# Encoder layer on one core: the order of the work in front of the experts, with the gate projection in pieces between attention's steps

## The reference, cut to what matters

```python
n = rms_norm(h, mix_norm_g)
z = n @ w_in                     # 1024 x 2336, all groups' projections side by side
gq, gk, gv, gr, zf, zb, aq, ak, av = split_cols(z, IN_SPLITS)
# gated linear attention (GLA), 4 heads, chunks of 64, forward and backward
g_fwd = log_sigmoid(zf @ w_gf + b_gf) / 16      # zf, zb: 16 columns each
g_bwd = log_sigmoid(zb @ w_gb + b_gb) / 16
o = rms_norm(o_f + o_b, head_g) * silu(gr)      # gr: 512 columns, the output gate
# softmax attention, 8 query heads on 2 key heads, rotary positions
qf = axial_rope(rms_norm(qh, q_g)) * DH ** -0.5
kf = axial_rope(rms_norm(kh, k_g))
h = h + concat(o_gla, o_att) @ w_out            # 1024 x 1024
# mixture of experts: top 4 of 32, clamped SwiGLU, then a last norm
h = h + moe_ffn(rms_norm(h, ffn_norm_g), ...)
y = rms_norm(h, final_norm_g)
```

## Time and profile before

| | |
|---|---|
| median of 3 runs | 1078.08 us (1078.02 to 1078.13) |
| the profiled execution's own time | 1077.54 us |
| its span | 1075.5 us |
| PE busy | 984.4 us (92%) |
| DVE, ACT, POOL busy | 224.2, 117.7, 15.5 us |
| DMA | 421.4 MB, mean 392 GB/s |
| chain that ended last | PE 53%, DMA 39%, DVE 4%, ACT 2% |

### The profile page before, as it was taken

How to read it: one execution, slowest core, us unless ns; L and a number is a source line. 1 busy time by engine, 2 the same in 40 slices (tenths; PEclk the granted TensorE clock), 3 DMA queues, 4 the chain that set the end, 5 groups by cost and what they waited for, 6 DMA issues and landing times.

```text
span 1075.5 us, 13809 instructions
## 1 busy us (share of the span) xinstructions
PE 984.4 (92%) x5833; PEld 424.4 (39%) x5833; DVE 224.2 (21%) x522; ACT 117.7 (11%) x233; POOL 15.5 (1%) x19
## 2 busy tenths in 40 slices
PE   7997989999999999988888988898988888999996
PEld 4644543444444444333333333333333333333432
DVE  1577342111111111111111101111111111101112
ACT  1053130000000000000000000000000000000002
POOL 0010010000000000000000000000000000000000
PEclk9998899999999999999999999999999999999999
DMA  9924748999999999999999999999999999999995
GB/s 330 295 108 206 313 157 347 427 428 427 426 428 427 428 429 429 428 428 428 429 428 428 427 428 428 429 428 428 429 429 429 429 428 428 428 428 427 427 423 225
DMA packets 33675, 421.40 MB, mean 392 GB/s; under 512 B 4944, under 2 KB 5456, under 8 KB 7568
## 3 DMA queue, kind: packets, MB, share of 16 engines
q1 hardware_dynamic: 33648, 421.02, 93.6%
HBM read 419.95 MB, written 1.05 MB: 391 GB/s over the span
## 4 chain that ended last, share of the span: by engine, by line
PE 53%; DMA 39%; DVE 4%; ACT 2%; issue 1%; POOL 0%; SPq 0%; POOLq 0%
DMA ring<-in_w_dram 38%; PE bank L1534 22%; PE bank L1576 13%; PE bank L1148 4%; PE bank L1460 3%; PE bank L1448 3%; PE bank L1362 1%; PE bank L1558 1%; ACT work L606 1%; PE bank L1494 1%; PE bank L1354 1%; PE bank L1383 1%; ACT work L537 1%; DMA h<-in_x_dram 0%; PE bank L1290 0%
## 5 line engine op out<-in xcount | busy, mean ns | idle before, releaser
L1534 PE MATMUL bank<-ring,work 128*64 128x512 f32 x2016 | 457.4, 598 | 45.4 <-DMA ring<-in_w_dram 44.3
L1534 PEld LDWEIGHTS bank<-ring,work 128*64 128x64 f32 x2016 | 167.4, 136 | 315.3 <-issue 212.5
L1576 PE MATMUL bank<-ring,work 128*64 128x512 f32 x992 | 219.7, 595 | 15.1 <-ACT work L606 15.1
L1039 DVE TENSOR_SCALAR work<-bank 128x512 f32<-128x512 f32 x31 | 21.4, 692 | 697.4 <-PE bank L1534 697.4
L1576 PEld LDWEIGHTS bank<-ring,work 128*64 128x64 f32 x992 | 69.0, 137 | 145.8 <-issue 128.9
L603 ACT ACTIVATE work<-work 128x512 f32<-128x512 f32 x31 | 19.6, 632 | 512.1 <-DVE work L1039 512.1
L1460 PE MATMUL bank<-work 64*128 64x512 f32 x256 | 63.6, 615 | 0.7 <-ACT work L638 0.7
L1448 PE MATMUL bank<-work,tok 128*128 128x64 bf16 x992 | 46.7, 193 | 0.0
L1448 PE MATMUL bank<-work 128*128 128x64 bf16 x496 | 45.2, 194 | 0.0
L1448 PEld LDWEIGHTS bank<-work,tok 128*128 128x128 bf16 x992 | 43.7, 98 | 0.0
L614 ACT ACTIVATE work<-bank 128x512 f32<-128x512 f32 x31 | 18.5, 597 | 214.8 <-PE bank L1576 214.8
(11 more groups left out here) (212 smaller groups left out, 505.3 us busy)
## 6 DMA issues: line engine op xcount, KB each, us to landing
ring<-in_w_dram SPq DMA_DIRECT2D x187, 2048.0 KB, 33.1
ring<-in_w_in_dram SPq DMA_DIRECT2D x8, 1168.0 KB, 17.3
ring<-in_w_dram SPq DMA_DIRECT2D x6, 1024.0 KB, 33.2
work<-in_w_dram SPq DMA_DIRECT2D x2, 2048.0 KB, 11.3
ring<-in_w_out_dram SPq DMA_DIRECT2D x2, 1024.0 KB, 13.2
ring<-in_w_out_dram SPq DMA_DIRECT2D x1, 2048.0 KB, 19.5
h<-in_x_dram SPq DMA_DIRECT2D x2, 512.0 KB, 4.3
out_dram<-tok SPq DMA_DIRECT2D x4, 256.0 KB, 2.2
```

The costliest lines, as they stand in the source:

```text
L1039: nc.vector.tensor_scalar(glu, bank[2][:, :], LIMIT, None, ALU.min).then_inc(S.glu_ready, 1)
L1534: last = mm(bank[(2, 5)[g]][j * CAP:(j + 1) * CAP, :], xg[:, k * CAP:(k + 1) * CAP], chunk[:, r, g * FF + j * FG:g * FF + (j + 1) * FG], s ...
L1576: last = mm(bank[6][j * CAP:(j + 1) * CAP, :], hidT[:, r, s * CAP:(s + 1) * CAP], chunk[:, r, j * 512:(j + 1) * 512], start=s == 0 and r == 0,
```

## The change

The same arithmetic, in another order, and in other banks:
- **Pass 1.** The low-rank columns are made with the activations stationary (128 wide) and the 32 weight columns moving, for both t, and come out with tokens on partitions (bank 1). DVE scales them by the row's 1/rms (`zg_t`), PE turns them back (`turn_zg`, two transposes), DVE copies them into `zg`. Attention's q of t = 1 leaves pass 1 and becomes eight matmuls behind it, with `turn_zg` after the first and `gates()` after the fourth.
- **Gate pass.** Pass 3 is cut into pieces of 4, 2 and 2 k (`gate_pass`), which lie between attention's steps; ACT copies its result out (`gate_out`, Copy in place of Sigmoid), the sigmoid comes later, after attention.
- **`turn_qk`** moves into pass 2, behind k = 5; the rotation on DVE (`rotated(0)`, `rotated(1)`) moves ahead of the scans of the gate chain; ACT's squares for q and k go into a buffer of their own (`sq`) and ahead of Abs, Exp, Ln.
- **GLA's products** on DVE are cut up (`decayed_near`, `decayed_queries`, `decayed_keys`, `carried_keys`) and lie between the softmax steps. `gla_first(0)` comes after `turn_weights(2)`.
- **Output projection.** Attention's part (`out_att`) lies in part between attention's steps and GLA's outputs; all of it, for t = 1 too, is ahead of the wait for `ogla_sb`.
- **Waits.** The router's and GLA's late constants have a semaphore of their own (`late_in`), so `const_in` counts four transfers in place of six. The early chunks wait for `mix01_used` in place of `attT_ps`.

```diff
-CONSTS = 6
+CONSTS = 4
+LATE = 2
...
-            sp.wait_ge(S.attT_ps, ATT_PAIRS)
+            sp.wait_ge(S.mix01_used, 1)
...
+            act.wait_ge(S.raw_sb, 3 * TILES)
+            nc.scalar.activation(sq, raw, ACT.Square).then_inc(S.raw_sq, 1)
...
+            def gate_out():
+                act.wait_ge(S.pass3, KD)
+                for t in range(TILES):
+                    nc.scalar.activation(sg[:, t, :], bank[MIX[t]][:, :], ACT.Copy, scale=stat[:, 4 + t:5 + t]).then_inc(S.gr_sb, 1)
...
+            for t in range(TILES):
+                nc.scalar.activation(tok[:, t, GLA_V:D], sg[:, t, :], ACT.Sigmoid).then_inc(S.gr_sig, 1)
...
+            dve.wait_ge(S.raw_sb, 3 * TILES)
+            step(rotated(1))
+            dve.wait_ge(S.raw_sq, 1)
+            step(nc.vector.tensor_reduce(stat[:, 28:48], sq.rearrange("p t (h d) -> p (t h) d", d=DH), AX.X, ALU.add))
+            mean_eps(stat[:, 8:28], stat[:, 28:48], DH).then_inc(S.hvar_done, 1)
+            step(nc.vector.tensor_tensor(rot, rot, swp, ALU.add))
             dve.wait_ge(S.gln, 1)
             step(nc.vector.scalar_tensor_tensor(gM, gM, 0.0, gA, ALU.min, ALU.subtract))
+            dve.wait_ge(S.hrstd_done, 1)
...
+            decayed_near()
+            row_maxima(0)
+            row_maxima(1)
+            normalise(0)
+            decayed_queries()
+            weights_out(0)
+            decayed_keys()
+            normalise(1)
+            carried_keys()
+            row_maxima(2)
+            weights_out(1)
+            normalise(2)
+            row_maxima(3)
+            weights_out(2)
+            normalise(3)
+            dve.wait_ge(S.late_in, 16 * LATE)
+            gla_scores(0)
+            weights_out(ATT_PAIRS - 1)
+            gla_scores(1)
...
-                put(bank[2][0:2 * RANK, 0:SEQ], w[:, C_ZG:C_AQ], xT(k), True)
+                for t in range(TILES):
+                    last = put(bank[1][:, t * 2 * RANK:(t + 1) * 2 * RANK], xT(k, t), w[:, C_ZG:C_AQ], t == 0)
...
+            for k in range(KD):
+                last = mm(bank[4][:, :], xT(k, 1), w_in_sb[:, k, C_AQ:C_AK], start=k == 0, stop=k == KD - 1)
+                if k == 0:
+                    turn_zg()
+                if k == 3:
+                    gates()
+            last.then_inc(S.pass1, 1)
...
-            pe.wait_ge(S.rms_sb, 1)
+            pe.wait_ge(S.gates_sb, 1)
             for k in range(KD):
                 for t in range(TILES):
                     last = mm(bank[6 + t][:, :], xT(k, t), w_in_sb[:, k, C_GV:C_GR], start=k == 0, stop=k == KD - 1)
                 last.then_inc(S.pass2, 1)
-                if k == 0:
-                    gates()
+                if k == 5:
+                    turn_qk()
+
+            def gate_pass(k0, k1):
+                if k0 == 0:
+                    pe.wait_ge(S.gqk_sb, 2)
+                for k in range(k0, k1):
...
-            pe.wait_ge(S.raw_sb, 3 * TILES)
-            for k in range(KD):
-                for t in range(TILES):
-                    last = mm(bank[3 + t][:, :], xT(k, t), w_in_sb[:, k, C_GR:C_ZG], start=k == 0, stop=k == KD - 1)
-                last.then_inc(S.pass3, 1)
-                if k == KD - 3:
-                    turn_qk()
...
             scores(0)
-            gla_first(0)
             scores(1)
+            gate_pass(0, 4)
             turn_weights(0)
-            gla_second(0)
+            gate_pass(4, 6)
             values(0)
             scores(2)
             turn_weights(1)
-            gla_first(1)
+            gate_pass(6, 8)
             values(1)
             scores(3)
             turn_weights(2)
+            gla_first(0)
+            gla_second(0)
+            values(2)
+            pe.wait_ge(S.w_out_att_in, 32)
+            out_att(0, (0,))
+            turn_weights(3)
+            gla_first(1)
             gla_second(1)
-            turn_weights(3)
-            values(2)
+            values(3)
+            out_att(0, (1,))
+            pe.wait_ge(S.mix_done, 2)
             gla_outputs(0)
-            gla_outputs(1)
-            values(3)
+            gla_outputs(1).then_inc(S.mix01_used, 1)
             gla_outputs(2)
             gla_outputs(3).then_inc(S.ogla_ps, 1)
+            pe.wait_ge(S.attT_sb, 2)
+            out_att(0, (2, 3))
+            out_att(1, range(4)).then_inc(S.att_used, 1)
```

More of the change, by code:

```diff
@@ L178, in encoder_layer @@
         av = front(TILES, ATT_KV)
+        at_gv = front.at
         gv = front(TILES, GLA_V)
@@ L187, in encoder_layer @@
         picked = front(TILES, EXPERTS + TOP_K)
+        zg_t = front(TILES, 2 * RANK)
         assert front.at <= WORK
@@ L194, in encoder_layer @@
         rms = reuse(SEQ)
+        sq = Carve(work, at_gv)(TILES, QK)
+        assert at_gv + TILES * QK <= at_sg + SEQ
         reuse = Carve(work, at_rot)
@@ L796, in _ @@
-            step(last)
-            for d in range(2):
-                nc.vector.tensor_tensor(pairs(gB, d), pairs(gB, d), q2, ALU.mult).then_inc(S.gla_ready, 1)
-            k4 = k2.rearrange("p (g c i) -> p g c i", g=2, i=CHUNK)
-            for d in range(2):
-                last = nc.vector.tensor_tensor(kk[:, 2 * d:2 * d + 2, :, :].rearrange("p g s i -> p g s i")[:, :, 0:5:2, :],
-                                               gM[:, 2 * d:2 * d + 2, :].rearrange("p g (c i) -> p g c i", i=CHUNK)[:, :, d:d + 3, :],
-                                               k4[:, :, d:d + 3, :], ALU.mult)
@@ L805, in _, with decayed_near, decayed_queries @@
-            step(last)
+            def decayed_near():
+                dve.wait_ge(S.exp_done, 2)
+                for d in range(2):
+                    nc.vector.tensor_tensor(pairs(gX, d), pairs(gX, d), q2, ALU.mult).then_inc(S.gla_ready, 1)
+                    nc.vector.tensor_tensor(pairs(gA, d), pairs(gA, d), k2, ALU.mult).then_inc(S.gla_ready, 1)
+            dec = stat[:, 128:128 + 4 * CHUNKS]
+            def decayed_queries():
+                dve.wait_ge(S.exp_done, 4)
+                for d in range(2):
+                    last = nc.vector.tensor_copy(dec[:, 8 * d:8 * d + 8].rearrange("p (c o) -> p c o", o=1),
+                                                 chunked(gB, d)[:, :, edge[d]:edge[d] + 1])
+                step(last)
+                for d in range(2):
+                    nc.vector.tensor_tensor(pairs(gB, d), pairs(gB, d), q2, ALU.mult).then_inc(S.gla_ready, 1)
@@ new lines, in decayed_keys @@
+            def decayed_keys():
+                k4 = k2.rearrange("p (g c i) -> p g c i", g=2, i=CHUNK)
+                for d in range(2):
+                    last = nc.vector.tensor_tensor(kk[:, 2 * d:2 * d + 2, :, :].rearrange("p g s i -> p g s i")[:, :, 0:5:2, :],
+                                                   gM[:, 2 * d:2 * d + 2, :].rearrange("p g (c i) -> p g c i", i=CHUNK)[:, :, d:d + 3, :],
+                                                   k4[:, :, d:d + 3, :], ALU.mult)
+                step(last)
@@ L811, in carry, with carried_keys @@
                                                dec4[:, d, :, c:c + 1].broadcast_to([P, 2, CHUNK]), ALU.mult)
[L813 to L825 removed]
+            def carried_keys():
+                carry(0, 1, 0, 1)
+                carry(0, 6, 2, 2)
+                carry(1, 5, 2, 1)
+                step(carry(1, 3, 4, 2))
+                carry(0, 5, 1, 2)
+                carry(1, 6, 3, 1).then_inc(S.kk_done, 1)
             def row_maxima(i):
@@ L1344, in router_sum @@
                     .then_inc(S.logit_ps, 1)
-            pe.wait_ge(S.w_out_att_in, 32)
-            pe.wait_ge(S.attT_sb, 2)
-            for t in range(TILES):
-                if t == 1:
-                    pe.wait_ge(S.ogla_sb, TILES)
-                for k in range(4):
-                    for nb in range(2):
-                        last = mm(bank[Y[2 * t + nb]][:, :], xT(4 + k, t), w_out_att[:, k, nb * 512:(nb + 1) * 512],
-                                  start=k == 0, stop=False, skip_group_check=True)
-            last.then_inc(S.att_used, 1)
             pe.wait_ge(S.ogla_sb, TILES)
```

235 lines of the change are left out of this document (119 added, 116 removed).

## The result

The changed kernel takes 1061.12 us in the median of four runs (1060.22 to 1064.76), the kernel before on the same chip 1078.11 (1078.02 to 1080.27): a ratio of 0.9841, interval 0.9822 to 0.9860. The forecast was 1064.1 with a range of 1060.5 to 1070.5. The execution with the profile is the longest of the four, 1064.76 us with a span of 1062.6.

What follows compares the result with a forecast made beforehand. The DMA stream sets the end, a constant after PE's first chunk use; PE's front path comes 14.0 us earlier: 1077.54 - 14.0 = 1063.5, plus 0.5 for the median, 1064.1 us (rounded). Range 1060.5 to 1070.5.

Steps and rivals of the forecast that it cites:

- The bound: First chunk's use, at 164.7 us before: the end is that moment plus a constant, each us moved counting one.
- Rival 4: Whole kernel: the gain does not reach the end because DMA is the bound throughout, 1078 us; chance 3%.
- Pass 1: Front, PE: eight rounds of 4.22 us in place of 5.05, with 0.6 us for the norm's row, 34.4 us.
- "No wait" for w_in: Eight rounds at the front: block 4 lands at 27.9 us, PE comes to it at 28.0, later blocks have more room.
- Query, turning, gates: PE behind the eight rounds: query of t = 1, turning zg and gates take 9.1 us, ending at 54.7.
- Pass 2 and the rotation: Before attention: twelve matmuls, 10.3 us, then turned q and k copied by 70.8 us; PE waits 1.1 us.
- Rival 2: DVE or ACT later than walked, at turned q and k or one softmax, by 3 to 6 us: 1067 to 1070; 13%.
- Attention: PE from first scores at 70.8 us to GLA's turned output at 121.0, all four softmaxes covered by 0.8 to 1.6 us.
- Rival 1: Clock falls in the changed attention, 94 to 106 us at 1.2 GHz, up to 6 us longer: 1070; 14%.
- Rival 3: PE better: narrow matmuls near their columns' time, smaller wait at turned q and k, 2 to 3.5 us more: 1060.7 to 1062; 10%.
- The 0.5 us added for the median: Final sum: the median of the runs was taken as 0.5 us above the profiled execution, added to 1063.5.
- Rival 5: Front: 32-column matmuls do not keep the clock up, eight rounds at 1.2 GHz, net 20 us slower, 1098; 3%.

Runs made afterwards that it cites:

- 256-column form: Changed kernel with the low-rank columns of pass 1 made the old way again (32 weight columns stationary, 256 tokens moving): 1062.92 us, ratio 0.9844.
- the kernel with both edits: Changed kernel with bias rows issued behind w_in's sixth block and copies of turned q and k ahead of the edge differences on DVE: 1060.70 us, ratio 0.9841.

## Why the prediction was right, and where its numbers were off

- **The bound** (first chunk's use plus a constant): right, by the table. Rival 4, that DMA hides the gain, is out.
- **Pass 1**, 34.4 us forecast, 34.7 measured, but by luck: errors against each other. The round was over-priced: the four narrow records were taken at 0.128 us each, 0.51. Measured, 3.90 - (5.05 - 0.48 - 0.86) = 0.19 us for all four, near the lower end of 0.13; the 256-column form's round, 4.20, says the same (4.20 - 0.48 + 0.19 = 3.91). The step that failed is the choice of the row: L1290's record has 128 columns of its own to pass, and the full loading was taken to be paid besides. And "No wait" for w_in was wrong: PE came to block 4 earlier, and in this execution the block landed past 30 us, not at 27.9. In the traces of the changed order with the bias rows where the change has them, PE got that block between 28.0 and 31.0 us wherever it waited for it. One landing time of one execution was used as if it were fixed. The first ten records, 2.80 us in place of 2.33, added 0.5 more. The page TensorE: Matmul & The Clock Gate of the Trainium skill (LDWEIGHTS), with 107 ns for a 128-wide load, gives 0.43 us for the four; it was nearer than my 0.51, but the trace lies under it, so the loads did not bind here.
- **Query, turning, gates:** 9.1 forecast, 55.65 - 46.44 = 9.2 measured.
- **Pass 2 and the rotation:** scores at 70.8 forecast, 72.89 measured. Of the 2.1 us, 0.95 was there at the start of pass 2, 0.66 of it since pass 1 began at 11.76 and not at 11.1; 0.8 is POOL's power, 4.71 us and not 3.91, and the rest lies in hand-overs of 0.1 to 0.2 us between ACT, DVE and POOL that the walk left out. The wait became 1.6 + 0.5, not 1.1. Rival 2 thus came in at about 1 us, not at its 3 to 6.
- **Attention:** 50.2 forecast (70.8 to 121.0), 48.7 measured. The covers were 0.8 to 1.6 us on paper and all held. The first scores took 1.9 (forecast 2.2), each of GLA's two double steps 98.28 - 95.83 = 2.45 (2.8), GLA's outputs 3.73 (4.05). The clock is not the difference, for the rows read for these forecasts stood at a granted 0.98 to 1.00 as well. Scores and outputs now each come in one unbroken stream, where the rows were those of two pieces, and the 0.4 us that had been added to GLA's 2.4 did not appear.
- **Rival 1**, the clock falling in attention: out, 1.00 from 80 to 140. The experiments show when it does fall: behind gaps of 4.1, 3.6 and 12.2 us, and of 3.0 us in pass 1. That agrees with the rule cited with the rival. The length of one gap does not settle it, though: in the kernel before, the clock also read 0.50 from 111 to 114 us behind a gap of 1.7 us (to 110.94), and in the changed one it stayed at 1.00 behind 1.56 us. It fell in one place that I had not priced, the short steps ahead of the first expert: 0.74 and 0.57 in two windows of 5 us, where in the same work before it was 0.95 and 0.71 (153.54 to 158.54 and to 163.54 us), 0.65 us more in the first sixteen records.
- **Rival 3**, PE better: this is where the median lies. Half of its condition came true, the narrow matmuls near their columns' time; the other half did not, for the wait at the turned q and k was larger than forecast. The profiled execution is 1.3 us above its forecast of 1063.5; the other three are 1.8 to 3.3 us under, and none of them has a trace. Other traces show things of this size that vary: a start at 10.5 in place of 11.8, a wait for w_in of 0.4 us or none, first sixteen records of 4.1 to 4.3 us. Which of them the faster three had is open. The 0.5 us added for the median had the wrong sign: three runs of the kernel before lay within 0.1 us, but on the three chips of the experiments it spread over 5 to 9.5 us, so its small spread was luck as well.
- **Rival 5:** out; pass 1 at 3.90 a round.

## What to carry to other kernels

Where an engine waits in a chain of short steps, move long independent matmuls in pieces between the steps: pieces of 7.1 and 3.6 us were enough here for softmax chains of about 5 us that had begun earlier, and they keep the clock up as well, which was a third of what the gate pieces gave (2.7 of 8.1 us). Then look at the order on the *unbusy* engine: the rotation's place on DVE was worth 13 us, more than either of the two moves on PE that were undone, PE's order being the changed one each time. Before costing a cheaper matmul, ask which landing comes next, and take the spread of that landing, not one value.

## What I had not expected of the hardware

- Four float32 records with 32 moving columns and a 128-wide stationary operand cost 0.19 us in a stream of wide ones, where two by themselves took 0.31.
- POOL's 20-element power took 4.71 us in the changed kernel and in the run with the rotation late, where DVE does a 1280-wide addition beside it, and 3.91 before, where a 512-wide product stands there. The difference, 0.80 us, is that of the two DVE operations, 1.48 against 0.68 us, as if POOL were held until DVE's is through. The page GPSIMD Engine Reference of the Trainium skill (Specifications) has POOL share its SBUF interfaces with VectorE, with contention for DVE instructions with two SBUF inputs, as both are. The rows agree only for the operation that is running when POOL starts: before, DVE went on with such products nearly all through POOL's 3.91 us, and it took less. No run took the DVE operation away, so the cause is open.
- In the kernel with both edits the first ten records of pass 1 took 4.48 us and in the other traces of this form 2.33 to 4.35, the same instructions at a granted clock that reads 1.00. What makes them slow is open.
- In one trace a wait of 3.0 us for w_in was followed by a granted clock of 0.66 and cost some 1.7 us more in that round. A late block can so cost more than its wait.
